# A two-block transformer kernel: the latent norms' scales moved behind the projections, the query rotation and one weight half moved in their queues

## The chip, the cores and the metric

The kernel runs on one core of a Trainium2 chip. The core has five engines that matter here: TensorE (PE in the rows; PEld is its weight load), VectorE (DVE), ScalarE (ACT), GpSimd (POOL) and the queue of SyncE (SP), which issues most DMAs. The metric is the device time of one execution in microseconds (us); lower is better. About 0.2% (5 us) is what a measurement of this kernel can tell from no change.

## The reference, cut to what matters

Two blocks are computed one after the other on 512 tokens of width 1024, in fp32. The first block has a forgetting attention ("fox", 8 heads), a stick-breaking attention (8 heads) and a mixture of 16 experts. The second block has two layers; the mixer of its first layer ("mixer a", the second mixer of the whole program) has a short convolution and a latent attention. Of mixer a the change touches this:

```python
proj = xn @ w_in
g_b, g_c, hv, c_q, c_kv, k_r = jnp.split(proj, [o1, o2, o3, o4, o5], axis=-1)
y_conv = g_b * short_conv(g_c * hv, conv_w)
q = (rms_norm(c_q, q_norm) @ w_q_up).reshape(b, s, MLA_HEADS, MLA_NOPE + MLA_ROPE)
q = jnp.concatenate([q[..., :MLA_NOPE], rope(q[..., MLA_NOPE:], pos)], axis=-1)
kv = (rms_norm(c_kv, kv_norm) @ w_kv_up).reshape(b, s, MLA_HEADS, MLA_NOPE + MLA_V)
k_rope = jnp.broadcast_to(rope(k_r[:, :, None, :], pos), (b, s, MLA_HEADS, MLA_ROPE))
```

with `rms_norm(x, g) = x * rsqrt(mean(x*x) + EPS) * g`. `c_q` has 768 features, `c_kv` 256, `k_r` 32. The root mean square is one number per token, and a projection sums over features, so it can be multiplied in before or behind the projection.

## The kernel before

Each engine has one instruction queue written out by hand; semaphores order the engines, and nothing is scheduled by a planner. PSUM has 8 banks, `PB[0]` to `PB[7]`, of 128 x 512 fp32. They are used as two sets, 0 to 3 and 4 to 7. A product of 512 x 512 outputs is a "group" with a running number; even groups write set 0, odd ones set 1. `acc_done` counts the groups that TensorE has completed, `acc_free[s]` the evictions of set s (ScalarE evicts set 0 and VectorE set 1 in most stages), and TensorE waits for it before it writes the set again (`await_set`).

Most products are made of split operands: a weight chunk arrives in `RING` by DMA, ScalarE casts half a chunk to its high part `WH` (`split` on ScalarE, line 893), VectorE subtracts to get the low part `WL` (`split` on VectorE, line 2376), and TensorE runs three matmuls for each pair of tiles (`split_group`, line 1578). Such a half chunk is called a part; a group has four parts of 24 matmuls. In both queues `upto(n)` issues the splits of the parts below n that are still to come. `WH` and `WL` have two buffers, so ScalarE casts part q when part q-1 has begun.

**The end of fox attention** (lines 2619 to 2657, and 1834 to 1841 on TensorE). TensorE computes group g+4 (parts 12 to 15). Behind part 14 it runs `last_spreads`: two matmuls that write the inverse softmax sums to `PB[7]`, one after the other, each followed by a gather on VectorE (`fox_gather`, line 2614). Then comes part 15. VectorE has in its queue: the low half of part 14, gathers 2 and 3, four multiply-adds of the modulation (`ada_part`), the low half of part 15, four more multiply-adds, and the low half of part 16, the first one of group g+5.

**Mixer a.** Its input projection has six groups: g to g+4 are split groups for `GBT`, `GCT`, `HVT` and the latents (g+3: tiles 0 to 3 of `CQ`; g+4: tiles 4 and 5 of `CQ` and both of `CKV`), feature-major, that is with tokens along the columns. Group g+5 is the 32 features of `k_r`: 64 plain fp32 matmuls of 32 columns into `PB[4]` (line 2066). Then comes the latent norm: ScalarE squares `CQ` and `CKV` into `SQ`; TensorE multiplies by a matrix of ones (lines 2074 and 2078), which leaves the sum over features in all 128 partitions, for 512 tokens along the columns; VectorE and ScalarE take mean, root and reciprocal on 128 x 512 tiles (`RT`), and VectorE scales the eight tiles in place, with the gain as a per-partition scalar (lines 2960 to 2969). `l_c` then lets TensorE start the projections `qup` (two groups) and `kvup` (two groups), whose outputs have tokens in the partitions (`QN`, `KVN`). `rope` rotates the queries in `QN` and VectorE's last eviction fills the second half of `KVN`; GpSimd copies the keys' parts from `KVN` and `KR2` to `KN` (lines 1476 to 1483). TensorE then transposes queries (`m = 0`) and keys (`m = 1`) by heads (line 2127), and VectorE and ScalarE evict them alternately. The attention loop `mla` follows.

A plain fp32 matmul has two records in the trace, a transpose or a split matmul has one.

## Time and profile before

| | us |
|---|---|
| median of 3 runs | 2497.91 (2496.5 to 2499.46) |
| the profiled execution, whole | 2497.15 |
| span of its trace | 2495.1 |
| TensorE busy in it | 2279.3 |
| VectorE busy | 1237.6 |
| ScalarE busy | 929.9 |
| GpSimd busy | 182.7 |

Times inside the trace count from the start of the span. The rest of the execution lies around it. The granted TensorE clock is given as a share of 2.4 GHz: 1.00 is 2.4 GHz, 0.50 is 1.2 GHz. The profile's chain of work goes back from the last instruction, at each step to what released it; where a wait is named after one engine, another may have come as late.

### The profile page before, as it was taken

The page shows a single profiled execution, that of the slowest core. Times are in us where ns is not written, and L with a number is a line of the kernel's source. Part 1 is how long each engine was busy: PE and PEld are TensorE (multiplying, and loading weights), DVE is VectorE, ACT ScalarE, POOL GpSimd, SP SyncE. Part 2 cuts the span into 40 slices and gives each one's busy share as a digit, 9 for nine tenths or more (in the row PEclk, how much of TensorE's full clock was granted, in tenths as well). Part 3 has the DMA queues.
Part 4 walks back from the last instruction along what each step waited for, and adds up shares of the span by engine and source line. Part 5 has one row for each costly group of instructions (what it writes and reads, how often), then busy time and mean ns, then how long its engine had stood idle before and what let it go on. Part 6 is the DMA issues. An engine that isn't in the chain of part 4 may idle for free.

```text
span 2495.1 us, 26080 instructions
## 1 busy us (share of the span) xinstructions
PE 2279.3 (91%) x10140; PEld 1712.4 (69%) x10140; DVE 1237.6 (50%) x1672; ACT 929.9 (37%) x1433; POOL 182.7 (7%) x222
## 2 busy tenths in 40 slices
PE   6898999987999959977889999989999997899998
PEld 4667667656666637845678888878855556788887
DVE  5735543256777744244554444453345545444544
ACT  3443531134555523203451224342255453312343
POOL 0330001101000010001000000020211200000000
PEclk9999899988999979978999999999899998999999
DMA  9303124827999952210123233232100002233221
GB/s 360 102 11 135 35 96 149 331 76 290 368 375 372 383 208 85 72 48 32 34 77 101 86 100 101 92 113 85 36 1 1 1 1 68 79 99 101 93 93 68
DMA packets 148459, 309.38 MB, mean 124 GB/s; under 512 B 17774, under 2 KB 19699, under 8 KB 148341
## 3 DMA queue, kind: packets, MB, share of 16 engines
q1 hardware_dynamic: 120468, 229.75, 27.0%
q10 hardware_dynamic: 16500, 36.62, 4.3%
q0 software_dynamic: 11376, 41.42, 4.2%
q8 instruction: 79, 1.29, 0.2%
q14 instruction: 36, 0.29, 0.0%
HBM read 276.56 MB, written 30.99 MB: 123 GB/s over the span
## 4 chain that ended last, share of the span: by engine, by line
PE 78%; DVE 10%; DMA 4%; ACT 4%; issue 3%; ACTq 0%; POOL 0%; DVEq 0%; POOLq 0%; SPq 0%; PEldq 0%
PE PB L1576 51%; PE PB L2020 4%; PE PB L2285 3%; DMA BIG<-in_expert_w_down 3%; PE PB L1561 2%; PE PB L2261 1%; DVE WL L2379 1%; PE PB L2089 1%; PE PB L2066 1%; PE PB L1802 1%; PE PB L2262 1%; DVE CI L3131 1%; PE PB L2224 1%; DVE X L2439 1%; PE PB L1723 1%
## 5 line engine op out<-in xcount | busy, mean ns | idle before, releaser
L2379 DVE TENSOR_TENSOR WL<-RING,WH 128x1024 fp32r<-128x1024 f32 x232 | 286.9, 1236 | 660.4 <-ACT WH L899 384.2
L899 ACT CAST WH<-RING 128x1024 fp32r<-128x1024 f32 x232 | 244.9, 1056 | 873.4 <-PE PB L1576 848.9
L1576 PE MATMUL PB<-HTH,WH 128*128 128x512 f32 x1056 | 416.8, 395 | 15.5 <-DVE WL L2379 9.7
L1576 PE MATMUL PB<-HTL,WH 128*128 128x512 f32 x1056 | 414.0, 392 | 0.0
L1576 PE MATMUL PB<-HTH,WL 128*128 128x512 f32 x1056 | 413.7, 392 | 0.0
L1576 PEld LDWEIGHTS PB<-HTH,WH 128*128 128x128 f32 x1056 | 200.3, 190 | 61.5 <-DVE WL L2379 12.1
L1576 PEld LDWEIGHTS PB<-HTH,WL 128*128 128x128 f32 x1056 | 200.1, 189 | 41.9
L1576 PEld LDWEIGHTS PB<-HTL,WH 128*128 128x128 f32 x1056 | 200.2, 190 | 41.6 <-issue 0.7
L1576 PE MATMUL PB<-WH,NHH 128*128 128x512 f32 x512 | 199.4, 390 | 1.8 <-DVE NHL L2382 1.8
L1576 PE MATMUL PB<-WH,NHL 128*128 128x512 f32 x512 | 199.2, 389 | 0.0
L1576 PE MATMUL PB<-WL,NHH 128*128 128x512 f32 x512 | 199.2, 389 | 0.0
L2746 DVE TENSOR_TENSOR EWL<-RING,EWH 128x1024 fp32r<-128x1024 f32 x128 | 151.8, 1221 | 59.7 <-ACT EWH L1093 59.5
L1576 PE MATMUL PB<-EWH,HTL 128*128 128x512 f32 x512 | 169.5, 413 | 3.9 <-DVE HTL L2888 3.9
L1093 ACT CAST EWH<-RING 128x1024 fp32r<-128x1024 f32 x128 | 130.6, 1049 | 92.1 <-PE PB L1576 70.7
L1576 PE MATMUL PB<-WH,HTH 128*128 128x512 f32 (+1 forms) x320 | 123.1, 385 | 23.7 <-DVE HTL L2382 16.0
L1576 PE MATMUL PB<-WH,HTL 128*128 128x512 f32 (+1 forms) x320 | 121.2, 379 | 0.0
L1576 PE MATMUL PB<-WL,HTH 128*128 128x512 f32 (+1 forms) x320 | 120.7, 377 | 0.0
L1576 PEld LDWEIGHTS PB<-EWH,HTL 128*128 128x128 f32 x512 | 95.8, 192 | 28.5 <-issue 6.7
L1576 PEld LDWEIGHTS PB<-WH,NHH 128*128 128x128 f32 x512 | 96.1, 188 | 22.5 <-DVE NHL L2382 2.6
L2020 PE MATMUL PB<-BIG,NAT 128*128 128x512 f32 x240 | 106.1, 594 | 4.8 <-DMA BIG<-in_expert_w_down 4.6
L1576 PEld LDWEIGHTS PB<-WL,NHH 128*128 128x128 f32 x512 | 96.1, 188 | 20.1
L1576 PEld LDWEIGHTS PB<-WH,NHL 128*128 128x128 f32 x512 | 96.1, 188 | 19.8
(497 smaller groups left out, 3491.1 us busy)
## 6 DMA issues: line engine op xcount, KB each, us to landing
RING<-in_mlp_w SPq DMA_DIRECT2D x64, 1024.0 KB, 5.2
RING<-in_expert_w_gate SPq DMA_DIRECT2D x32, 1024.0 KB, 7.4
RING<-in_expert_w_up SPq DMA_DIRECT2D x32, 1024.0 KB, 11.9
BIG<-in_expert_w_down ACTq DMA_DIRECT2D x15, 2048.0 KB
BIG<-in_ada_w SPq DMA_DIRECT2D x10, 2048.0 KB, 11.0
RING<-in_w_in SPq DMA_DIRECT2D x20, 1024.0 KB, 5.2
dispatch_rows<-BIG POOLq DMA_DIRECT2D x24, 512.0 KB, 16.0
RING<-in_a_w_in SPq DMA_DIRECT2D x10, 1024.0 KB, 5.1
```

What stands on the lines that cost most here:

```text
L899: ins = nc.scalar.copy(WH[:, q % 2], halves_of(n, q))
L1093: nc.scalar.copy(EWH[:, q % MOE_SLOTS], halves_of(CH["moe"] + GU_AT[e] + j // 2, j)).then_inc(high_ready, 1)
L1561: ins = pe.matmul(PB[4 * (g % 2) + b][:, :], lhs, rhs, start=(opens and m == 0 and k == 0), stop=(closes and m == chunks - 1 and k == KK - 1))
L1576: yield pe.matmul(dst, lhs, rhs, start=(start and n == 0), stop=(stop_ and n == 2))
L1723: ins = pe.matmul(PB[6 + u % 2][:, 0:DH], PT[0:n, u % 2, j, :], v(it, h, b, j, n), start=(j == 0), stop=(j == len(m) - 1))
L1802: ins = pe.matmul(PB[5 + h % 2][:, j * P:T], v, PROB[:, n % 4, 0:T - j * P], start=(j == 0), stop=(j == NT - 1))
L2020: ins = pe.matmul(PB[5 + m][:, :], ACTT[e % 2][:, k, :], w[:, k, :], start=(k == 0), stop=(k == KK - 1))
L2066: ins = pe.matmul(PB[4][:, i * 32:(i + 1) * 32], x[:, k, i * P:(i + 1) * P].bitcast(F32), SW[:, k, SW_KR:SW_KR + 32], start=(k == 0 and n ...
L2089: ins = pe.matmul(PB[b][:, :], CQ[:, k0 + k, b * P:(b + 1) * P], w[:, k, :], start=(m == 0 and k == 0), stop=(m == 1 and k == kk - 1))
L2285: ins = pe.matmul(dst, lhs, rhs, start=(j == 0), stop=last)
L2379: ins = V.tensor_tensor(WL[:, q % 2], halves_of(n, q), WH[:, q % 2].bitcast(F32), ALU.subtract)
L2746: V.tensor_tensor(EWL[:, q % MOE_SLOTS], halves_of(CH["moe"] + GU_AT[e] + j // 2, j), EWH[:, q % MOE_SLOTS].bitcast(F32), ALU.subtract).th ...
```

## The change

In mixer a, the latents are evicted from PSUM with their gain already multiplied in (`latents` on VectorE), and ScalarE squares the raw sums straight from PSUM (`latent_squares`). The per-token sums are no longer spread over all partitions: each of 32 matmuls takes 128 tokens of one tile of squares as the stationary operand and two columns of ones as the moving one, so that the sums come out with tokens in the partitions, all in `PB[5]`. Mean, root and reciprocal are taken on 128 x 8 numbers (`LSUM`, `LRMS`, `LRSTD`). The reciprocal root is multiplied in when the projections are evicted, as a per-partition scale (`evac` with `scale`, on both engines). TensorE starts `qup` when the latents have been evicted. In VectorE's queue `rope` of the queries now stands ahead of the eviction of the second `kvup` group. Near the end of fox attention the low half of part 15 is split ahead of gathers 2 and 3, and the release of the PSUM set stands ahead of the modulation's multiply-adds.

```diff
@@ ScalarE, mixer a
+            upto(18)
+            def latent_squares(m):
+                act.wait_ge(acc_done, g + 4 + m)
+                for b in range(4):
+                    ins = nc.scalar.activation(LSQ[:, 4 * m + b, :], PB[4 - 4 * m + b][:, :], ACT.Square)
+                ins.then_inc(l_sq, 1)
+            latent_squares(0)
             upto(20)
-            evac(g + 4, lambda b: CQ[:, 4 + b, :] if b < 2 else CKV[:, b - 2, :])
-            act.wait_ge(acc_free[0], (g + 4) // 2 + 1)
-            act.wait_ge(acc_free[1], (g + 4) // 2)
-            nc.scalar.activation(SQ[...][:, 0:6, :], CQ, ACT.Square).then_inc(l_sq, 1)
-            nc.scalar.activation(SQ[...][:, 6:8, :], CKV, ACT.Square).then_inc(l_sq, 1)
-            for m in range(2):
-                act.wait_ge(l_ms, m + 1)
-                nc.scalar.activation(RT[:, m, :], RT[:, m, :], ACT.Sqrt).then_inc(l_rms, 1)
-            evac(GR["qup"], lambda b: QN[:, b, 0:W])
-            evac(GR["kvup"], lambda b: KVN[:, b, 0:W])
+            latent_squares(1)
+            act.wait_ge(l_ms, 1)
+            nc.scalar.activation(LRMS, LSUM, ACT.Sqrt).then_inc(l_rms, 1)
+            act.wait_ge(l_c, 2)
+            evac(GR["qup"], lambda b: QN[:, b, 0:W], scale=lambda b: LRSTD[:, b:b + 1])
+            evac(GR["kvup"], lambda b: KVN[:, b, 0:W], scale=lambda b: LRSTD[:, NT + b:NT + b + 1])
@@ TensorE, mixer a
-            pe.wait_ge(acc_free[0], (g + 1) // 2)
-            pe.wait_ge(l_sq, 1)
-            for k in range(6):
-                ins = pe.matmul(PB[0][:, :], ONES[:, 0:P], sq[:, k, :], start=(k == 0), stop=(k == 5))
-            ins.then_inc(l_sum, 1)
             pe.wait_ge(l_sq, 2)
-            for k in range(2):
-                ins = pe.matmul(PB[1][:, :], ONES[:, 0:P], sq[:, 6 + k, :], start=(k == 0), stop=(k == 1))
+            for i in range(NT):
+                for at_, tiles in ((i, range(6)), (NT + i, (6, 7))):
+                    for k in tiles:
+                        ins = pe.matmul(PB[5][:, 2 * at_:2 * at_ + 2], LSQ[:, k, i * P:(i + 1) * P], ONES[:, 0:2],
+                                        start=(k == tiles[0]), stop=(k == tiles[-1]))
             ins.then_inc(l_sum, 1)
@@ VectorE, end of fox attention
-            upto(15)
+            upto(16)
             fox_gather(2)
             fox_gather(3)
-            ada_part(0, 3, ADA_ACC[4], 0, 4, fresh=True)
             dve.wait_ge(f_used, 4)
             dve.sem_inc(acc_free[1], 1)
-            upto(16)
+            ada_part(0, 3, ADA_ACC[4], 0, 4, fresh=True)
             ada_part(0, 3, ADA_ACC[4], 4, 4)
             upto(17)
@@ VectorE, mixer a
-            evac(g + 3, lambda b: CQ[:, b, :])
+            latents(0, [(CQ, "a_q_norm_2", k) for k in range(4)])
             upto(20)
...
+            latents(1, [(CQ, "a_q_norm_2", k) for k in (4, 5)] + [(CKV, "a_kv_norm_2", k) for k in (0, 1)])
+            dve.wait_ge(acc_free[0], (g + 4) // 2 + 1)
+            dve.sem_inc(l_c, 1)
+            dve.wait_ge(acc_done, g + 6)
+            V.tensor_copy(KRN.rearrange("p a b -> p (a b)"), PB[4][:, 0:NT * 32])
+            dve.wait_ge(l_sum, 1)
...
+            dve.wait_ge(l_ms, 1)
+            dve.sem_inc(acc_free[1], 1)
+            dve.wait_ge(l_rms, 1)
+            V.reciprocal(LRSTD, LRMS).then_inc(l_c, 1)
...
-            evac(GR["qup"] + 1, lambda b: QN[:, b, W:768], width=256)
-            evac(GR["kvup"] + 1, lambda b: KVN[:, b, W:D])
+            evac(GR["qup"] + 1, lambda b: QN[:, b, W:768], width=256, scale=lambda b: LRSTD[:, b:b + 1])
             dve.wait_ge(acc_free[0], GR["qup"] // 2 + 1)
+            dve.wait_ge(acc_free[1], (GR["qup"] + 1) // 2 + 1)
             rope(QN.rearrange("p t (h d) -> p t h d", h=MLA_H), MLA_H, None).then_inc(m_qn, 1)
+            evac(GR["kvup"] + 1, lambda b: KVN[:, b, W:D], scale=lambda b: LRSTD[:, NT + b:NT + b + 1])
```

Three places in the engines' queues. First VectorE at the end of fox attention, before; `WL<-RING,WH` is the low half of a part, `FOT<-FOT,PB` a gather, `NAT<-BIG,STAT` the modulation's multiply-adds:

```order
L2612 TENSOR_TENSOR FWT<-FSUMS,FWT 4x512 [waits dve_chain]
L2379 TENSOR_TENSOR WL<-RING,WH 128x1024 [waits high_parts_written]
L2617 TENSOR_TENSOR FOT<-FOT,PB 128x512 [waits fox_weights_spread] x2
L2358 TENSOR_SCALAR NAT<-BIG,STAT 128x512 [waits ada_pair_in0]
L2360 SCALAR_TENSOR_TENSOR NAT<-BIG,STAT,NAT 128x512 [waits dve_chain] x3
L2379 TENSOR_TENSOR WL<-RING,WH 128x1024 [waits dve_chain,fox_weights_used,high_parts_written]
L2360 SCALAR_TENSOR_TENSOR NAT<-BIG,STAT,NAT 128x512 [waits ada_pair_in0]
L2360 SCALAR_TENSOR_TENSOR NAT<-BIG,STAT,NAT 128x512 [waits dve_chain] x3
L2379 TENSOR_TENSOR WL<-RING,WH 128x1024 [waits high_parts_written]
```

The same place in the changed kernel:

```order
L2615 TENSOR_TENSOR FWT<-FSUMS,FWT 4x512 [waits dve_chain]
L2382 TENSOR_TENSOR WL<-RING,WH 128x1024 [waits high_parts_written] x2
L2620 TENSOR_TENSOR FOT<-FOT,PB 128x512 [waits fox_weights_spread] x2
L2361 TENSOR_SCALAR NAT<-BIG,STAT 128x512 [waits fox_weights_used,ada_pair_in0]
L2363 SCALAR_TENSOR_TENSOR NAT<-BIG,STAT,NAT 128x512 [waits dve_chain] x3
L2363 SCALAR_TENSOR_TENSOR NAT<-BIG,STAT,NAT 128x512 [waits ada_pair_in0,dve_chain]
L2363 SCALAR_TENSOR_TENSOR NAT<-BIG,STAT,NAT 128x512 [waits dve_chain] x3
L2382 TENSOR_TENSOR WL<-RING,WH 128x1024 [waits high_parts_written]
```

The low half of part 15 moved ahead of both gathers, and all eight multiply-adds now stand between the gathers and the low half of part 16.

Second, TensorE between the products for `k_r` and the first `qup` group, before:

```order
L2074 MATMUL PB<-NAT,ONES 128x512 [waits latent_squares,acc_free0]
L2074 MATMUL PB<-NAT,ONES 128x512 x5
L2078 MATMUL PB<-NAT,ONES 128x512 [waits latent_squares]
L2078 MATMUL PB<-NAT,ONES 128x512
L2089 MATMUL PB<-RING,BIG 128x512 [waits chunk_in_slot0,latent_normed,acc_free0]
```

And in the changed kernel:

```order
L2080 MATMUL PB<-ONES,NAT 128x2 [waits latent_squares]
L2080 MATMUL PB<-ONES,NAT 128x2 x31
```

Eight wide matmuls became 32 narrow ones; the `qup` products follow them at once, with `latent_normed` (`l_c`) already raised by the evictions of the latents.

Third, VectorE from the projections' evictions to the evictions of the transposed heads, before:

```order
L2453 COPY NAT<-PB 128x256 [waits acc_done,dve_chain]
L2453 COPY NAT<-PB 128x256 x3
L2453 COPY HT<-PB 128x512 [waits acc_done]
L2453 COPY HT<-PB 128x512 x3
L2982 TENSOR_TENSOR BIG<-NAT,COS 128x512 [waits acc_free0]
...
L2988 TENSOR_TENSOR NAT<-BIG 128x32x16 [waits dve_chain]
L3011 TENSOR_SCALAR BIG<-PB 96x512 [waits mla_transposed] x4
```

And in the changed kernel:

```order
L2458 TENSOR_SCALAR NAT<-PB,STAT 128x256 [waits acc_done,dve_chain]
L2458 TENSOR_SCALAR NAT<-PB,STAT 128x256 x3
L2995 TENSOR_TENSOR BIG<-NAT,COS 128x512 [waits acc_free1,acc_free0]
...
L3001 TENSOR_TENSOR NAT<-BIG 128x32x16 [waits dve_chain]
L2458 TENSOR_SCALAR HT<-PB,STAT 128x512 [waits acc_done]
L2458 TENSOR_SCALAR HT<-PB,STAT 128x512 x3
L3025 TENSOR_SCALAR BIG<-PB 96x512 [waits mla_transposed] x4
```

The seven steps of the rotation moved ahead of the four evictions into `KVN` (`HT`).

## Rows read from the trace of the kernel before

**Rows 1.** The page: busy time of each engine; the chain's shares by engine.
```profile
PE 2279.3 (91%) x10140; PEld 1712.4 (69%) x10140; DVE 1237.6 (50%) x1672; ACT 929.9 (37%) x1433; POOL 182.7 (7%) x222
...
PE 78%; DVE 10%; DMA 4%; ACT 4%; issue 3%; ACTq 0%; POOL 0%; DVEq 0%; POOLq 0%; SPq 0%; PEldq 0%
```

**Rows 2.** Chain of waits, fox's end: start us, us, engine, tile, line, count.
```profile
194.87 16.58 PE PB L1576 x72
...
212.55 0.49 PE PB L1781
...
216.68 1.24 DVE WL L2379
217.96 8.20 PE PB L1576 x24
```

**Rows 3.** Timeline of VectorE there: start us, us, line, operation, count, [idle before].
```profile
213.06 0.69 DVE L2617 TENSOR_TENSOR FOT<-FOT,PB 128x512 f32<-128x512 f32 x1 [0.66 <-PE PB L1781]
213.66 0.48 DVE L2358 TENSOR_SCALAR NAT<-BIG,STAT 128x512 f32<-128x512 f32 x1
214.18 2.33 DVE L2360 SCALAR_TENSOR_TENSOR NAT<-BIG,STAT,NAT 128x512 f32<-128x512 f32 x3
...
217.82 3.11 DVE L2360 SCALAR_TENSOR_TENSOR NAT<-BIG,STAT,NAT 128x512 f32<-128x512 f32 x4
```

**Rows 4.** Timeline of ScalarE there: the cast of part 15.
```profile
206.33 1.06 ACT L899 CAST WH<-RING 128x1024 fp32r<-128x1024 f32 x1 [4.38 <-PE PB L1576]
```

**Rows 5.** Windows there: length, busy PE, PEld, DVE, ACT, POOL, clock, DMA share, GB/s.
```profile
213.00:218.00 5.00, 0.06 (x2) 0.04 (x1) 4.66 (x7) 0.00 (x0) 0.00 (x0) 0.84 0.00 0
218.00:226.00 8.00, 8.00 (x25) 6.35 (x26) 3.96 (x5) 1.05 (x1) 0.00 (x0) 0.67 0.01 2
```

**Rows 6.** Chain of waits in mixer a, from the k_r products to the keys' transposes.
```profile
1050.67 22.11 PE PB L2066 x128
1072.78 7.17 PE PB L2074 x12
1079.95 1.72 PE PB L2078 x4
1081.67 12.90 issue
1094.57 23.75 PE PB L2089 x48
...
1128.68 13.75 PE PB L2111 x32
...
1142.45 2.48 DVE HT L2453 x4
...
1150.78 5.78 PE PB L2127 x32
...
1157.42 3.69 PE PB L2127 x32
```

**Rows 7.** A window in mixer a; columns as in rows 5.
```profile
1056.00:1072.50 16.50, 16.50 (x80) 16.50 (x79) 0.00 (x0) 0.52 (x1) 0.00 (x0) 0.50 0.00 1
```

**Rows 8.** Windows of 2 us where the clock rises again; columns as in rows 5.
```profile
1076.00:1078.00 2.00, 2.00 (x5) 0.91 (x4) 0.00 (x0) 0.00 (x0) 0.00 (x0) 0.86 0.00 0
...
1100.00:1102.00 2.00, 2.00 (x6) 0.87 (x5) 1.90 (x4) 0.00 (x0) 0.00 (x0) 0.89 0.51 207
```

**Rows 9.** Line 1629, two-column matmuls: min/median/max ns, first to last start us.
```profile
L1629 PE MATMUL PB<-ONES,SCORE x16: 251/251/272, 37.9 to 39.6; 128*128 128x2 f32 x16
```

**Rows 10.** Timeline of VectorE in mixer a: a reciprocal, and the convolution's end.
```profile
1082.31 3.34 DVE L2964 RECIPROCAL BIG<-BIG 128x512 f32<-128x512 f32 x1
...
1106.72 0.69 DVE L3002 TENSOR_TENSOR BIG<-BIG 128x512 f32<-128x512 f32 x1
```

**Rows 11.** GpSimd's two copies for the keys: min/median/max ns, first to last start us.
```profile
L1481 POOL COPY BIG<-HT x4: 922/1068/1074, 1145.1 to 1150.1; 128x512 f32<-128x512 f32 x4
...
L1482 POOL COPY BIG<-BIG x4: 397/718/855, 1146.0 to 1151.1; 128x256 f32<-128x256 f32 x4
```

More of the change, by code:

```diff
@@ L368, in program @@
     KRN, KR2, RT = big(10240, NT, 32), big(10368, NT, 32), big(10496, 3, 512)
-    OT2, SQ = big(6144, 4, T), NAT
+    OT2, LSQ = big(6144, 4, T), NAT[:, :, :].rearrange("p a (c b) -> p (a c) b", c=2)
     QN = NAT[:, :, :].rearrange("p a b -> p (a b)")[:, 0:NT * 768].rearrange("p (a b) -> p a b", a=NT)
@@ L677, in program @@
         PRMS, PRSTD, EPS2 = STAT[:, 50:54], STAT[:, 54:58], STAT[:, 49:50]
+        LSUM, LRMS, LRSTD = (STAT[:, 32 + 8 * i:40 + 8 * i] for i in (0, 1, 3))
         SQX = PT[:, :, :, :].rearrange("p a b c -> p (a b c)")
@@ L910, in evac @@
                 for b in range(banks):
-                    ins = nc.scalar.activation(dst(b), PB[b][:, 0:width], func, scale=scale)
+                    ins = nc.scalar.activation(dst(b), PB[b][:, 0:width], func, scale=scale(b) if callable(scale) else scale)
                 ins.then_inc(acc_free[0], 1)
@@ L2954, in _, with latents @@
             upto(18)
[L2955 to L2969 removed]
+            def latents(m, tiles):
+                dve.wait_ge(l_sq, m + 1)
+                for b, (dst, name, k) in enumerate(tiles):
+                    at_ = VEC_AT[name] + k
+                    ins = V.tensor_scalar(dst[:, k, :], PB[4 - 4 * m + b][:, :], COLS[:, at_:at_ + 1], None, ALU.mult)
+                ins.then_inc(acc_free[1 - m], 1)
+            latents(0, [(CQ, "a_q_norm_2", k) for k in range(4)])
+            upto(20)
+            latents(1, [(CQ, "a_q_norm_2", k) for k in (4, 5)] + [(CKV, "a_kv_norm_2", k) for k in (0, 1)])
[4 more added lines that the diff above has]
+            dve.wait_ge(l_sum, 1)
+            for m, rank in enumerate((Q_RANK, KV_RANK)):
+                ins = V.tensor_scalar(LSUM[:, m * NT:(m + 1) * NT], PB[5][:, 2 * m * NT:2 * (m + 1) * NT:2], 1.0 / rank, EPS,
+                                      ALU.mult, ALU.add)
+            ins.then_inc(l_ms, 1)
+            dve.wait_ge(l_ms, 1)
+            dve.sem_inc(acc_free[1], 1)
+            dve.wait_ge(l_rms, 1)
+            V.reciprocal(LRSTD, LRMS).then_inc(l_c, 1)
+            dve.wait_ge(l_c, 2)
             def rope(v, heads, out_):
```

16 lines of the change are left out of this document (1 added, 15 removed).

## The prediction

> **What bounds the kernel now.** I read the page first: TensorE is busy for 91% of the span, and the chain of work that ended last runs through it for 78% [rows 1]. So an edit on another engine counts only where TensorE waits for it. I then read the chain of waits in the two stretches that the change touches. Near the end of fox attention the reader is to see that the chain leaves TensorE: the second spread ends at 213.04, and part 15 starts only at 217.96, released by VectorE's low half [rows 2]. In mixer a there are two more holes: 12.90 us between the sums and the first `qup` product, and 8.3 us from the end of `kvup` (1142.4) to the first transpose (1150.78) [rows 6]. The windows of the same stretches are the third view: they show at which clock TensorE works beside these holes [rows 5, 7, 8].
>
> **Part 1, the weight half ahead of the gathers.** ScalarE's cast of part 15 is done at 207.4 [rows 4], while VectorE next has work only for gather 2, behind TensorE's part 14. So the subtraction of 1.24 us fits ahead of the gathers and costs nothing; part 15 can start when the second spread ends, at 213.0 instead of 217.96. It has 24 matmuls. Before, it ran mostly at 1.2 GHz, since TensorE had been idle for 4.9 us (granted clock 0.67 from 218 to 226), and took 8.20 us [rows 2, 5]. The 72 matmuls of the three parts ahead took 16.58 us, so 24 take 5.5 us at 2.4 GHz. Part 15 then ends at 218.5.
>
> What is late next: part 16. Its low half stands behind all eight multiply-adds now. They start at 213.7 behind gather 3 and take 0.48 + 2.33 + 3.11 = 5.9 us [rows 3], then the subtraction takes 1.24 [rows 2]: 220.9. ScalarE's cast for it waits only for part 15 to begin. Before, part 16 began when part 15 ended, at 226.16. So this edit gives 226.16 - 220.9 = 5.2 us, while TensorE idles for 2.4 us ahead of part 16. The lower bound: should the clock fall in that gap, part 16 costs what part 15 did, 8.20 - 5.5 = 2.7 us more, which leaves 2.5. I take 5.2, since the gap is half of the one in which it fell before. Behind it all engines and the weight loads are triggered by TensorE's progress, so I expect the shift to be kept.
>
> **Part 2, the sums and the norm.** Removed from TensorE's path are the wide sums, 7.17 + 1.72 us, and the hole of 12.90 us, in which VectorE took two reciprocals of 128 x 512 (3.34 us each [rows 10]) and scaled eight tiles. The sum of what goes is 21.8 us [rows 6].
>
> Added are 32 narrow matmuls, 64 records. Their price depends on the clock. The 64 products of 32 columns for `k_r` run just ahead: in the windows from 1056 to 1072.5 they have 80 records in 16.5 us, 0.206 us each, at a granted clock of 0.50, though TensorE is never idle [rows 7]. At 2.4 GHz the two-column matmuls of line 1629 have 15 spacings in 1.7 us, 0.113 us each [rows 9]. The moving side being 2 columns instead of 32, I expect no less work, since 32 and 2 columns cost the same at 2.4 GHz to within the rounding. So the new sums cost 64 x 0.206 = 13.2 us at 1.2 GHz (13.7 if a few of the 80 lie partly outside the window) and 7.2 us at 2.4 GHz. I take 13.4: the narrow stream ahead was at 1.2 GHz to its end, and this one is narrower. Thus `qup` starts at 1072.78 + 13.4 = 1086.2 instead of 1094.57: 21.8 - 13.4 = 8.4 us gained (8.1 to 8.6).
>
> The Trainium skill (TensorE: Matmul & The Clock Gate, LDWEIGHTS) says that a weight load takes a time that goes by the columns of the stationary tile alone, and this speaks against the change: each narrow matmul still loads 128 columns, four times as often as the eight wide ones did. The rows agree in that 2 columns cost 0.113 us each. By the page's figure of 128/1.2 ns = 107 ns for a load, an estimate of the 64 would be 6.8 us, half of what I take for the lower clock.
>
> Work that leaves other queues' paths: ScalarE squares eight banks from PSUM and VectorE evicts with the gain. For g+3 this lies beside group g+4; for g+4 it lies beside the 22.11 us of `k_r` products. The mean, root and reciprocal on 128 x 8 numbers are tiny. The rotation of `k_r` and the convolution, which ended at 1107.4, 12.8 us behind the norm [rows 6, 10], now start at about 1087.5 and end at about 1101, ahead of the first `qup` eviction (1110). Without that cover, an eviction would be late by the part of the 12.8 us that sticks out. The set 1 banks are released when VectorE has read the sums, at about 1087, and the second `qup` group needs them 23 us later.
>
> `qup` itself took 23.75 us, of which the first 5.6 ran at 1.2 GHz: the clock rose inside the window from 1100 to 1102 [rows 6, 8]. In the sums before, it rose inside the window from 1076 to 1078, 3.7 us behind the first wide matmul [rows 8]. The new `qup` also starts at 1.2 GHz. I take no difference (bounds 0 and 1 us gained).
>
> **Part 3, the rotation ahead of the last eviction.** Call K the end of `kvup`. Before, VectorE evicted for 2.5 us behind K and then rotated; the transposes of the queries began at K+8.4 and those of the keys at K+15.0 [rows 6]. Now the rotation (5.9 us, from 1144.9 to 1150.8) lies beside the 13.75 us of `kvup` [rows 6]. The transposes of heads 0 to 3 start at K (0.46 us a head, 3.69 / 8), those of heads 4 to 7 behind the eviction, which is still at K+2.5 to K+2.8, and they are all evicted at about K+5.7. Then the keys: GpSimd's eight copies cannot start before the eviction has ended, as before (K+2.7). Before they took 6.45 us, from 1145.1 to 1151.5, and were hidden; now they are what ends last. The four 256-wide ones took 0.855 us beside VectorE's steps and 0.397 at the end without them [rows 11]. So the copies take 4 x 1.0 + 4 x 0.4 = 5.6 us now, when VectorE reads PSUM or rests (upper bound 6.45), and the keys' transposes start at K+8.5 (8.3 to 9.2) instead of K+15.0: 6.5 us.
>
> The Trainium skill (SBUF — State Buffer, Who interferes with whom) has a rule for this: a VectorE instruction with two SBUF inputs contends with a GpSimd instruction that reads SBUF, one with at most one does not. The trace agrees with its 0.855 and 0.397. Without the rule the copies would keep their 6.45 us, and the keys would start at K+9.2.
>
> The clock takes some of it back. TensorE idles from K+4.8 to K+8.5, so that I expect it to fall to 1.2 GHz around the keys' transposes. The same 32 transposes took 3.69 us at full clock and 5.78 us for the queries, mostly at the lower one [rows 6]: 2.1 us more, upper bound 3.7 (the double). So part 3 gives 6.5 - 2.1 = 4.4 us (2.1 to 6.5).
>
> **The sum** is 5.2 + 8.4 + 4.4 = 18.0 us. Against the profiled execution's span, 2495.1 becomes 2477.1, and the whole execution, 2497.15, 2479.2. The median of the runs is 0.8 us above that execution: 2497.9 - 18.0 = 2479.9.
>
> **Rivals.** *The clock falls twice more* (chance 0.20): in the 2.4 us ahead of part 16, and for all of the keys' transposes. It costs 2.7 + 1.6 us: 2484.2. For it: the clock is down after every idle stretch of 5 us or more. Against: here they are 2.4 and 3.7 us.
>
> *The clock comes sooner* (0.15): no fall around the keys, and `qup` at full speed 1 us earlier. That is 2.1 + 1 us less: 2476.8.
>
> *The narrow sums run at 2.4 GHz* (0.05): 64 x 0.113 = 7.2 us instead of 13.4, and `qup` without its slow start, 2.8 us less: 2479.9 - 9.0 = 2470.9. Against it stand the `k_r` products, back to back and at 0.50 [rows 7]. The Trainium skill (TensorE: Matmul & The Clock Gate, Loop structure matters more than you think) has matmuls that stay back to back stay at the full clock, which would lead here; this trace disagrees for narrow ones.
>
> *The change does not do what it says* (0.03): the holes only move, because the multiply-adds hold part 16 longer than worked out or the KN copies start late; less than 5 us is left, 2493 or more.
>
> *Slower* (0.03): one long run at the lower clock. With the hole gone, nothing separates the narrow stream from the projections, and if 1.2 GHz stayed granted through `qup` and `kvup`, they would take twice their full-clock time (21 + 10.4 + 13.7 us, of which 2.8 are lost already): 42 us more, 2522. It decides from 36 us more of the lower clock on. Against it: both wide streams of the rows were back at full clock 4 to 6 us after they began, one of them straight behind `k_r` [rows 8].
>
> My forecast as worked out holds 0.54 (2477.5 to 2482.5).
>
> **How the numbers follow.** The range for 8 in 10 takes in the forecast, the two clock cases and the bounds of the single terms: least gain 2.5 + 8.1 + 2.1 = 12.7 (2485.2), most 5.2 + 8.6 + 6.5 + 1 = 21.3 (2476.6); with about 1 us for the scatter of the median it is 2475.5 to 2486. Faster by over 0.2% (5 us; a measurement of this kernel can tell no less from no change): 0.94. Within 0.2%: 0.03. Slower: 0.03.
>
> **What would show it.** Part 1: part 15 starts at once behind the second spread, part 16 about 2.4 us after part 15's end, at clock 1.00. Part 2: 64 narrow records in 13 to 14 us at 0.50, `qup` at once behind, about 8.4 us sooner after the `k_r` products than before. Part 3: first transpose at K, GpSimd's copies some 5.6 us long, keys' transposes at K+8.5. Wrong would be: records of 0.11 us in the sums, a fall of the clock in part 16, an eviction of `qup` that waits for the convolution, or a later stretch that gives the shift back.

## The result, and the profile after

| | before | after |
|---|---|---|
| median of 4 runs, us | 2497.20 | 2472.27 (2470.48 to 2476.08) |
| ratio | | 0.9902, 95% interval 0.9889 to 0.9916 |
| the profiled execution, us | 2497.15 | 2476.08 |
| span of its trace, us | 2495.1 | 2474.0 |

The changed kernel is 24.9 us faster; the prediction was 2479.9, at least 2475.5. The direction and the three gains were as predicted; the size was larger, and the median lies 3.2 us below the range. The two profiled spans differ by 21.1 us, so 3.8 us of the 24.9 are not in this pair of profiles.

The page of the changed kernel answers to [rows 1]. Where line numbers differ from the rows of before, the operation and the tile name the same step: split matmuls L1582, `k_r` L2072, sums L2080, `qup` L2092 and L2102, `kvup` L2114, head transposes L2130.

```profile
PE 2274.8 (92%) x10188; PEld 1716.3 (69%) x10188; DVE 1225.9 (50%) x1667; ACT 925.4 (37%) x1434; POOL 180.4 (7%) x222
...
PE 79%; DVE 9%; DMA 5%; ACT 4%; issue 2%; POOL 1%; ACTq 0%; DVEq 0%; POOLq 0%; SPq 0%; PEldq 0%
```

TensorE has 48 records more and 4.5 us less busy time; GpSimd, which was at 0% of the chain, has 1%. That last point is the one that the prediction missed: a wait for GpSimd is now on the path.

**End of fox attention.** The chain of waits of the changed kernel (start us, us, engine, tile, line), which answers to [rows 2, 3]:

```profile
215.25 0.48 PE PB L1787
...
217.11 0.76 DVE NAT L2363
...
222.59 1.14 DVE WL L2382
...
223.87 8.19 PE PB L1582 x35
```

Its windows, which answer to [rows 5] (length, busy PE, PEld, DVE, ACT, POOL, clock, DMA share, GB/s):

```profile
213.00:218.00 5.00, 4.13 (x19) 3.10 (x18) 2.71 (x5) 1.05 (x1) 0.00 (x0) 1.00 0.13 50
218.00:223.00 5.00, 3.20 (x15) 2.31 (x13) 4.82 (x7) 1.74 (x3) 0.00 (x0) 1.00 0.00 0
```

The second spread ends at 215.73 and TensorE goes on at once with part 15; the chain runs along VectorE's multiply-adds to part 16 at 223.87. The clock is 1.00 through the whole place, where it was 0.84 and 0.67. This execution was 2.7 us later than that of before when it came here, and nearly all of that from near its start (the first matmul of L1748, ahead of fox attention, began at 95.0; its like of before at 92.4), so 223.87 compares with 226.16 + 2.7: 5.0 us gained. From the last spread to the first scores of the stick-breaking attention it took 53.0 us instead of 58.3: 5.3.

**Mixer a.** The chain of waits there, which answers to [rows 6]:

```profile
1068.12 13.61 PE PB L2080 x64
1081.72 23.02 PE PB L2092 x48
1104.75 10.36 PE PB L2102 x48
1115.11 13.75 PE PB L2114 x32
1128.88 2.74 DVE HT L2458 x4
...
1134.50 0.55 POOL BIG L1487
...
1135.39 6.63 issue
...
1142.46 1.02 POOL QS L1427
...
1143.74 2.43 PE PB L1708 x6
```

The 12.90 us of "issue" ahead of `qup` are gone. At the end of the stage there is a new "issue" of 6.63 us, between GpSimd's last copy for the keys and its copy of the first heads (`QS`), which the attention loop needs.

TensorE, VectorE and GpSimd behind K, the end of `kvup` (1128.88), in the timeline of the changed kernel; it answers to [rows 11]:

```profile
1131.75 0.61 POOL L1487 COPY BIG<-HT 128x512 f32<-128x512 f32 x1 [120.90 <-DVE HT L2458]
1132.31 0.39 POOL L1488 COPY BIG<-BIG 128x256 f32<-128x256 f32 x1
...
1135.45 3.70 PE L2130 MATMUL PB<-IDENT,BIG 128*96 128x128 f32 x32 [1.83 <-POOL BIG L1488]
...
1139.18 0.69 DVE L3027 COPY BIG<-PB 96x512 f32<-96x512 f32 x1 [0.19 <-PE PB L2130]
...
1142.43 1.04 POOL L1427 COPY QS<-BIG 96x1024 f32 x1 [7.04 <-POOLq L258]
```

The keys' transposes start at K+6.6 and take 3.70 us, at full clock. The last eviction ends at 1139.9, but `QS` starts 2.6 us later, released by line 258. That line is GpSimd's drain, in the helper `meet`, in which all engines wait for each other ahead of the attention loop (one line of before and one of after, min/median/max ns and first start):

```profile
L258 POOLq DRAIN  x3: 41/988/12749, 1145.3 to 2002.6; - x3
```
```profile
L258 POOLq DRAIN  x3: 41/987/9936, 1132.0 to 1981.7; - x3
```

The drain starts with the copies, at 1132.0, and its 9.9 us end at about 1142, some 6.5 us behind the last of them. Before, its 12.7 us from 1145.3 also ended 6.5 us behind the last copy (1158.0 against 1151.5), but there the transposes and evictions covered it: `QS` then started at 1162.3, 0.5 us behind the last eviction.

Where the 21.1 us between the two spans lie, from the starts of TensorE's groups: up to the last spread -2.7 (later); from there to the stick-breaking scores 5.3; to the experts' first down product 1.3; through the experts to the `k_r` products 0.4; from these to the last transpose behind the latent attention (called the last head transpose below) 16.4 (172.8 us to 156.4); behind it 0.4. Of the 16.4, 8.5 are the sums and the norm (start of `k_r` to start of `qup`, 43.9 to 35.4 us), 0.7 `qup`, 6.3 the way from K to the first matmul of the loop (21.2 to 14.9 us), and 0.8 the loop.

### The profile page after: what moved, and what is told of

Read it like the earlier page. It is cut to its first block, busy times and chain, and to the rows that moved or that the text cites. A ratio compares the mean times of both kernels' runs of the same rounds, so it can differ in the third digit from the quotient of the medians.

```text
span 2474.0 us, 26175 instructions
## 1 busy us (share of the span) xinstructions
PE 2274.8 (92%) x10188; PEld 1716.3 (69%) x10188; DVE 1225.9 (50%) x1667; ACT 925.4 (37%) x1434; POOL 180.4 (7%) x222
## 4 chain that ended last, share of the span: by engine, by line
PE 79%; DVE 9%; DMA 5%; ACT 4%; issue 2%; POOL 1%; ACTq 0%; DVEq 0%; POOLq 0%; SPq 0%; PEldq 0%
PE PB L1582 51%; PE PB L2026 4%; PE PB L2288 3%; DMA BIG<-in_expert_w_down 3%; PE PB L1567 2%; PE PB L2264 1%; DVE WL L2382 1%; PE PB L2092 1%; PE PB L2072 1%; PE PB L1808 1%; PE PB L2265 1%; DVE CI L3145 1%; PE PB L2227 1%; DVE X L2442 1%; DVE NAT L2363 1%
## 5 line engine op out<-in xcount | busy, mean ns | idle before, releaser
L1582 PE MATMUL PB<-HTH,WH 128*128 128x512 f32 x1056 | 416.3, 394 | 13.3 <-DVE WL L2382 7.6
L1582 PE MATMUL PB<-HTL,WH 128*128 128x512 f32 x1056 | 413.7, 392 | 0.0
L1582 PE MATMUL PB<-HTH,WL 128*128 128x512 f32 x1056 | 413.5, 392 | 0.0
L1582 PEld LDWEIGHTS PB<-HTH,WH 128*128 128x128 f32 x1056 | 200.1, 189 | 58.3 <-issue 10.9
L1582 PEld LDWEIGHTS PB<-HTL,WH 128*128 128x128 f32 x1056 | 200.1, 189 | 42.0 <-issue 0.7
L1582 PEld LDWEIGHTS PB<-HTH,WL 128*128 128x128 f32 x1056 | 199.9, 189 | 41.9
L1582 PE MATMUL PB<-WH,NHH 128*128 128x512 f32 x512 | 199.4, 389 | 1.7 <-DVE NHL L2385 1.7
L1582 PE MATMUL PB<-WH,NHL 128*128 128x512 f32 x512 | 199.2, 389 | 0.0
L1582 PE MATMUL PB<-WL,NHH 128*128 128x512 f32 x512 | 199.2, 389 | 0.0
L2748 DVE TENSOR_TENSOR EWL<-RING,EWH 128x1024 fp32r<-128x1024 f32 x128 | 151.6, 1219 | 59.8 <-ACT EWH L1094 59.7
L1582 PE MATMUL PB<-EWH,HTL 128*128 128x512 f32 x512 | 169.2, 412 | 3.9 <-DVE HTL L2890 3.9
L1582 PE MATMUL PB<-WH,HTH 128*128 128x512 f32 (+1 forms) x320 | 122.8, 384 | 23.6 <-DVE HTL L2385 16.0
L1582 PE MATMUL PB<-WH,HTL 128*128 128x512 f32 (+1 forms) x320 | 120.9, 378 | 0.0
L1582 PE MATMUL PB<-WL,HTH 128*128 128x512 f32 (+1 forms) x320 | 120.7, 377 | 0.0
L1582 PEld LDWEIGHTS PB<-EWH,HTL 128*128 128x128 f32 x512 | 95.2, 191 | 28.6 <-issue 6.7
L1582 PEld LDWEIGHTS PB<-WH,NHH 128*128 128x128 f32 x512 | 96.1, 188 | 22.5 <-DVE NHL L2385 2.6
L1582 PEld LDWEIGHTS PB<-WL,NHH 128*128 128x128 f32 x512 | 96.1, 188 | 20.1
L1582 PEld LDWEIGHTS PB<-WH,NHL 128*128 128x128 f32 x512 | 96.1, 188 | 19.7
```

What stands on the lines that cost most here:

```text
L1582: yield pe.matmul(dst, lhs, rhs, start=(start and n == 0), stop=(stop_ and n == 2))
L2748: V.tensor_tensor(EWL[:, q % MOE_SLOTS], halves_of(CH["moe"] + GU_AT[e] + j // 2, j), EWH[:, q % MOE_SLOTS].bitcast(F32), ALU.subtract).th ...
```

## The experiments

Theory: the three parts save what they saved in the trace, 5 + 9 + 6 to 7 us, and what goes beyond that in the first comparison is scatter in stretches that the change doesn't touch. Rivals: the parts help each other; the narrow sums cost something else than their length; GpSimd's drain holds back the third part. Kernels under one heading marked "same chip" were compared on one chip, with runs of the kernel before between them; the three groups below ran on three different chips.

**The change again, and its three parts alone (same chip).** The whole is the changed kernel. The other three are the kernel before with one part of the diff. Of fox, alone:

```diff
-            upto(15)
+            upto(16)
             fox_gather(2)
             fox_gather(3)
-            ada_part(0, 3, ADA_ACC[4], 0, 4, fresh=True)
             dve.wait_ge(f_used, 4)
             dve.sem_inc(acc_free[1], 1)
-            upto(16)
+            ada_part(0, 3, ADA_ACC[4], 0, 4, fresh=True)
```

The norm alone is the whole change with this place, and the order of `rope` and the last eviction, as before. The rotation alone:

```diff
-            evac(GR["kvup"] + 1, lambda b: KVN[:, b, W:D])
             dve.wait_ge(acc_free[0], GR["qup"] // 2 + 1)
+            dve.wait_ge(acc_free[1], (GR["qup"] + 1) // 2 + 1)
             rope(QN.rearrange("p t (h d) -> p t h d", h=MLA_H), MLA_H, None).then_inc(m_qn, 1)
+            evac(GR["kvup"] + 1, lambda b: KVN[:, b, W:D])
```

> The whole change again, to size the total. The profile of the changed kernel accounts for 20.6 us from the four gaps (5.1 at the end of fox attention, 8.5 at the sums, 0.7 in the first projection, 6.3 from the end of the projections to the attention loop). Theory (the parts add up and nothing else moved): 20 to 22 us below the kernel before on the same chip, ratio 0.9912 to 0.9920; the 24.9 us of the first comparison was then partly scatter of the medians. Rival (something outside the four gaps gives 3 to 4 us more): 24 to 25 us again, ratio about 0.990.

> The kernel before with the weight half of part 15 ahead of the gathers, and nothing else. Theory: part 15 starts at once behind the second spread and part 16 waits for the eight multiply-adds; 5.0 to 5.3 us faster, ratio 0.9979. Rival (the shift is given back by a later stage): 0 to 2 us. Rival (it is the source of the unexplained rest): 8 to 9 us.

> The kernel before with the latent norm's change alone: the rotation stays behind the last eviction, and the weight half behind the gathers. Theory: 64 narrow records in 13.6 us at clock 0.50, the projection at once behind; 8.5 + 0.7 = 9.2 us faster, ratio 0.9963. From the end of the projections to the attention loop it should take 21.2 us as before, with GpSimd's copies slow beside the rotation (about 1.0 us for the wide ones, 0.8 for the narrow ones). Rival (it is the source of the unexplained rest): 12 to 13 us.

> The kernel before with the queries' rotation ahead of the last eviction, and nothing else. Theory: GpSimd's copies take 0.60 and 0.39 us each, 3.6 us in all, since VectorE no longer has two operands in SBUF beside them; the keys' transposes start 6.6 us behind the projections' end instead of 15.0, GpSimd's drain ends 6.5 us behind its last copy and holds the attention loop until 14.9 us behind that end instead of 21.2: 6.3 us faster, ratio 0.9975. The prediction's own step had 4.4 us. Rival (the clock falls around the keys' transposes): 4 us.

| kernel (before: 2497.01, 22 runs) | median us | less than before | ratio, 95% interval | `k_r` to last head transpose |
|---|---|---|---|---|
| whole | 2483.10 (2477.62 to 2485.92) | 13.9 | 0.9943 (0.9930 to 0.9956) | 158.5 |
| fox alone | 2492.10 (2485.67 to 2500.03) | 4.9 | 0.9981 (0.9969 to 0.9994) | 173.0 |
| norm alone | 2487.27 (2482.06 to 2489.01) | 9.7 | 0.9957 (0.9945 to 0.9969) | 162.0 |
| rotation alone | 2490.74 (2486.87 to 2497.58) | 6.3 | 0.9975 (0.9965 to 0.9985) | 165.4 |

Each part alone is faster than before, by a median near what its place in the trace shows, and they add up to 20.9 us; the interval of each is about 3 us to either side. The parts don't help each other: in mixer a, norm and rotation alone save 10.8 and 7.4 us, both together 14.3 here and 16.4 in the three other profiles of the whole, so 2 to 4 us less than their sum. But the whole was only 13.9 us faster here, 11 less than in the first comparison and less than the 20 to 22 expected. At its own place fox alone does what part 1 said. The chain of that kernel:

```profile
219.77 1.14 DVE WL L2379
...
221.05 14.12 PE PB L1576 x61
```

Part 16 starts at 221.05; the prediction had worked out 220.9. In the total the same profile kept nearly nothing of it: the execution took 2496.97 us, its span 2494.9 against 2495.1. It began the stick-breaking scores at 265.5 us instead of 270.9, but the experts' first down product at 612.7 instead of 613.8. The stretch from the last stick-breaking product to that down product, first with fox alone, then before (length, busy engines, clock, DMA):

```profile
328.50:612.70 284.20, 251.01 (x965) 179.73 (x964) 122.07 (x196) 78.78 (x106) 29.28 (x44) 0.91 0.55 197
```
```profile
334.70:613.80 279.10, 247.72 (x966) 177.35 (x964) 121.23 (x196) 78.10 (x105) 29.37 (x44) 0.93 0.55 200
```

The eleven runs fall apart by their mean clock: five at 0.948 or 0.949 took 2485.67 to 2492.10 us, six at 0.943 to 0.945 took 2491.15 to 2500.03. The profiled one is of the six. It fits that the median of 4.9 us stands between executions that keep the gain and executions that give most of it back (the other ten have no profile), and its nearness to 5.2 is then partly luck. The rival "the shift is given back by a later stage" is true of the profiled execution.

GpSimd's timeline with the rotation alone, and with the norm alone (the rotation behind the eviction, as before):

```profile
1147.60 0.60 POOL L1481 COPY BIG<-HT 128x512 f32<-128x512 f32 x1
1148.15 0.39 POOL L1482 COPY BIG<-BIG 128x256 f32<-128x256 f32 x1
...
1156.49 1.04 POOL L1421 COPY QS<-BIG 96x1024 f32 x1 [7.04 <-POOLq L258]
```
```profile
1141.83 1.07 POOL L1487 COPY BIG<-HT 128x512 f32<-128x512 f32 x1
1142.85 0.59 POOL L1488 COPY BIG<-BIG 128x256 f32<-128x256 f32 x1
```

So it is the place of the rotation that sets the copies' length, 0.60 or 1.07 us for the same instruction. The rotation itself gets shorter too: its second step took 0.98 us before (1145.57) and 0.69 us in the kernel with the rotation alone. The Trainium skill (SBUF — State Buffer, Who interferes with whom) says that a VectorE instruction with two SBUF inputs contends with a GpSimd instruction that reads SBUF. The traces agree with it for the wide copies as well as for the small ones. But the rotation's one copy step, which has a single SBUF input, was slowed too, 0.72 us beside GpSimd's copies and 0.43 without, so the prediction's "one with at most one does not" is too wide.

**The drain, and the price of the narrow sums (same chip).** The whole once more; the whole without GpSimd's drain ahead of the loop, where GpSimd waits for its own last copy by semaphore instead:

```diff
-            meet(pool, "pool")
+            pool.wait_ge(m_kn, 1 + NT)
+            meets["pool"] = 1
+            pool.sem_inc(met, 1)
+            pool.wait_ge(met, 4)
```

The whole with all 32 sums computed twice:

```diff
-            for i in range(NT):
+            for again in range(2):
+              for i in range(NT):
```

And the whole with the narrow products mixed into `qup`: 24 of them go ahead, and three stand behind each of the 24 wide matmuls of the first `qup` group.

```diff
+            some(24)
...
                         ins = pe.matmul(PB[b][:, :], CQ[:, k0 + k, b * P:(b + 1) * P], w[:, k, :],
                                         start=(m == 0 and k == 0), stop=(m == 1 and k == kk - 1))
...
+                        some(3)
```

> The whole change a third time, since the two comparisons gave 24.9 and 13.9 us and the parts apart 4.9 + 9.7 + 6.3 = 20.9. Theory (executions of one program differ by where the clock's falls land in the stretch around the routing, from 330 to 620 us, and the first microseconds; the change's own four gaps are the same each time): the median lies between 2470 and 2486, and in the profile the stretch from the first k_r product to the end of the heads' transposes is 14 to 17 us shorter than the 172.8 us of the kernel before. Rival (the whole is faster than its parts by an interaction in mixer a): that stretch differs between profiles by more than the clock's low periods in it explain.

> The changed kernel, with GpSimd's drain ahead of the attention loop replaced by a wait on its own last copies. In the changed kernel that drain ends 6.5 us behind the last copy, at 14.9 us less 1.8 behind the projections' end, and the loop's first copy waits for it; all others are there 2.3 us sooner. Theory (the drain took the place of the wait that was removed): the loop starts 2.2 us sooner, 2 us faster than the whole change of this call. Rival (GpSimd is late for another reason, such as the fetch of its instructions): no difference, the gap ahead of the copy into QS stays.

> The changed kernel, with the order of TensorE's matmuls changed between the input projection and the query projection: 24 of the 96 narrow matmuls (64 for k_r, 32 for the sums) first, then three of them behind each of the 24 wide ones of the first qup group. Same matmuls, same waits. Theory (a stretch of narrow matmuls alone makes the clock fall, wide ones between them hold it up): clock 1.00 throughout, the 96 narrow ones take 96 x 0.224 = 21.5 us and the wide ones 20.7, so 42 us in place of 58.4 us from the first k_r product to the end of that group; 15 to 16 us faster than the whole change. Rival (the clock falls here anyway, as it goes by the share of narrow matmuls): up to 84 us, 26 us slower.

> The changed kernel with its 32 narrow sums done twice (the second overwrites the first). Theory (each costs two records of 0.213 us at 1.2 GHz, all on TensorE's path): 13.6 us slower than the whole change, 27.2 us for 128 records at clock 0.50. Rival (part of the sums is hidden, since the projection waits for something else too): less than 10 us.

| kernel (before: 2495.87, 23 runs) | median us | less than before | ratio, 95% interval |
|---|---|---|---|
| whole | 2477.04 (2473.99 to 2480.35) | 18.8 | 0.9925 (0.9909 to 0.9941) |
| without the drain | 2479.56 (2475.01 to 2483.13) | 16.3 | 0.9931 (0.9913 to 0.9948) |
| three narrow behind each wide one | 2498.91 (2457.26 to 2506.89) | -3.0 | not given, its 12 runs are of two kinds |
| sums twice | 2491.28 (2484.40 to 2496.42) | 4.6 | 0.9975 (0.9963 to 0.9988) |

*Sums twice* costs 14.2 us against the whole. The chain of waits shows why:

```profile
1069.12 27.26 PE PB L2081 x128
1096.38 23.17 PE PB L2093 x48
```

128 records in 27.26 us, 0.213 us each, twice the 13.61 us, and `qup` starts at once behind. So the narrow sums cost their length, at the lower clock, and nothing behind them.

*Without the drain* the tail got shorter in the trace. K is at 1134.96 there:

```profile
1141.55 3.71 PE PB L2133 x32
...
1146.49 1.02 POOL QS L1427
1147.77 0.93 PE PB L1711 x4
```

The loop starts at K+12.8 instead of K+14.9: the 2 us are there, so the drain did hold the loop back. One of them is lost again in the loop, which took 59.8 us from its first matmul to the last head transpose instead of 58.9, with a clock of 0.83 instead of 0.91 in its first 20 us. The median doesn't show the rest; it is 2.5 us worse than the whole, with overlapping runs, where 2 us better was expected. In its profile the windows of the experts' routing differ from those of the whole on the same chip (first the whole, then without the drain):

```profile
500.00:620.00 120.00, 93.90 (x426) 70.86 (x425) 74.77 (x139) 53.09 (x73) 11.59 (x11) 0.90 0.55 194
```
```profile
500.00:620.00 120.00, 95.64 (x412) 71.34 (x411) 71.57 (x135) 50.53 (x71) 11.00 (x11) 0.85 0.51 181
```

Up to there the two are the same program, and it ran at a clock of 0.90 or 0.85, depending on where the falls land. This window was read in eight profiles: four have 0.89 or 0.90, and four, the kernel before among them, 0.84 to 0.86. As it is fixed in time and the kernels are not, the length of the stage says more. From the last stick-breaking product to the first down product it took 277.8 to 279.1 us in nine of all fourteen profiles, and 281.4 to 284.2 in the other five. The nine reached the stage (the last stick-breaking product) at 330.3 us or later, the five at 329.8 or earlier, and all five have the fox edit. So the executions that come there earliest give 3 to 6 us back. No run moves the time of arrival alone, so that it is the cause is not shown. Half of the ten profiles with the fox edit and none of the four without it have the long stage: a gain of 2 us cannot be told from this in six runs. Whether the drain costs 2 us in the total is left open.

*Three narrow behind each wide one* was expected to be 15 to 16 us faster than the whole, with a clock of 1.00. Its median is 21.9 us slower: the prediction's rival "slower" made real. The clock in its windows:

```profile
1043.00:1053.00 10.00, 10.00 (x61) 8.00 (x60) 2.73 (x4) 2.06 (x4) 0.00 (x0) 0.77 0.18 52
1053.00:1070.00 17.00, 17.00 (x47) 11.32 (x48) 0.00 (x0) 0.00 (x0) 0.00 (x0) 0.50 0.08 32
1070.00:1090.00 20.00, 20.00 (x56) 13.28 (x56) 0.29 (x1) 0.00 (x0) 0.00 (x0) 0.50 0.00 0
1090.00:1110.00 20.00, 20.00 (x54) 12.77 (x53) 0.00 (x0) 0.00 (x0) 0.00 (x0) 0.50 0.16 53
```

Through the 57 us from 1053 to 1110 TensorE was never idle and had 1.2 GHz. The clock fell at the end of the 24 narrow products that go ahead (0.61 in the window 1048 to 1050; the first wide matmul began at 1048.2, 5.3 us behind the first narrow one), and the mixture did not bring it back. One of the 12 runs took 2457.26 us at a mean clock of 0.957 instead of 0.937 to 0.942. It has no profile; the clock alone suggests that in it the mixture ran at 2.4 GHz. The same program went both ways here.

**Without fox, and the narrow products among the split ones (same chip).** The whole a fourth time; the whole with the fox place as before; and two kernels in which a part of the 64 `k_r` products stands inside group g+4, one behind two of three wide matmuls (48 of them), or behind one of three (24), in the last three of its four parts:

```diff
+                                if between is not None and m > 0:
+                                    between((m - 1) * 24 + b * 6 + k * 3 + n)
...
+            def between(at_):
+                if at_ % 3 < 2:
+                    next(narrow, None)
```

`narrow` is a generator that issues the `k_r` products one by one, with the wait for set 1 ahead of the first; with 24, the 2 is a 1. The rest follows group g+4, and then the sums, as in the whole.

> The change as it is, a fourth time, as the partner of the others on this chip. If the differences between the earlier comparisons of it (13.9, 18.8 and 24.9 us) are scatter of the stretches that it does not touch: 2472 to 2484, and from the first record of line 2072 (1576 or 2066 as before) to the last head transpose 155 to 159 us, against 172.8 in the kernel before. If the gain in mixer a itself varied, that stretch would differ by 5 us or more.

> Only the second and the third part of the change: the order at the end of fox attention is that of the kernel before. If the fox edit is worth its 5 us in every run, this is 4 to 6 us slower than the whole on this chip, and 14 to 16 us faster than the kernel before. If most of the fox edit is taken back further on, in the stretch from 330 to 620 us, where the clock falls fall differently, it is within 2 us of the whole. Stretch from the k_r products to the last head transpose: 155 to 159 us in both theories.

> The whole change, but 48 of the 64 k_r products stand one by one behind two of every three wide matmuls in the last three parts of the last split group; 16 products and the 32 sums stay behind. If two narrow products to three wide matmuls leave the clock at 1.00, each product costs 2 x 0.113 us instead of 0.345 us and the narrow stream behind is 96 records long instead of 192, of which the first 4 us run at full clock: 10.8 + 4 + 12.6 = 27.4 us instead of 35.7, so 8 us faster than the whole. If such a mixture also pulls the clock down (as 3 narrow to 1 wide did), the 72 wide matmuls take up to 16 us more and the projections may start slowly too: 8 us slower than the whole, or more.

> As the one before, with one narrow product behind every third wide matmul: 24 of 64 between the wide ones, 40 behind. If the clock holds: 24 x 0.226 = 5.4 us instead of 8.3, so 3 us faster than the whole, and no fall before the last wide matmul. If even this pulls the clock down: 8 us or more slower. If it holds here and falls with 48 between, the share of narrow products decides; if it falls in neither or in both, a share in this range does not.

| kernel (before: 2497.82, 11 runs) | median us | less than before | ratio, 95% interval | last down product to last head transpose |
|---|---|---|---|---|
| whole | 2476.30 (2472.98 to 2480.18) | 21.5 | 0.9915 (0.9901 to 0.9929) | 303.7 |
| without the fox edit | 2483.41 (2477.67 to 2484.61) | 14.4 | 0.9940 (0.9926 to 0.9955) | 303.6 |
| 48 between | 2470.19 (2464.65 to 2470.68) | 27.6 | 0.9892 (0.9877 to 0.9906) | 295.6 |
| 24 between | 2476.23 (2473.08 to 2484.11) | 21.6 | 0.9918 (0.9902 to 0.9933) | 303.4 |

*Without the fox edit* it is 7.1 us slower than the whole in the medians, so here the fox edit keeps its worth; the two profiled executions, 2479.58 and 2480.65 us, differ by only 1.1. Its chain has part 15 late and slow again, as before:

```profile
219.19 1.24 DVE WL L2382
220.48 8.15 PE PB L1582 x24
```

Both profiles have the short stage ahead of the first down product. Behind it the shift does not stay whole. At the last stick-breaking product the kernel without the edit is 5.5 us behind, at the first down product 5.9 and at the last one 3.1: the experts' stretch took 292.8 us in the one and 290.0 in the other. Over the fourteen profiles it took 287 to 294 us, without a relation to the edits.

*48 between* is the fastest, faster than the whole by 6.1 us, and by 8.1 in the stretch from the last down product to the last head transpose. Its windows in the mixture and behind it:

```profile
1035.00:1040.00 5.00, 5.00 (x33) 4.48 (x33) 0.00 (x0) 0.47 (x1) 0.00 (x0) 1.00 0.00 0
...
1050.00:1055.00 5.00, 5.00 (x33) 4.48 (x32) 0.00 (x0) 0.00 (x0) 0.00 (x0) 1.00 0.00 0
1055.00:1060.00 5.00, 5.00 (x42) 4.76 (x40) 0.53 (x1) 2.06 (x4) 0.00 (x0) 1.00 0.02 3
1060.00:1065.00 5.00, 5.00 (x31) 5.00 (x31) 2.49 (x5) 0.00 (x0) 0.00 (x0) 0.62 0.00 0
1065.00:1070.00 5.00, 5.00 (x25) 5.00 (x25) 0.00 (x0) 0.00 (x0) 0.00 (x0) 0.50 0.00 0
```

And its chain behind the mixture:

```profile
1057.34 3.49 PE PB L2074 x32
1060.83 13.12 PE PB L2098 x64
1073.95 22.93 PE PB L2110 x48
```

Two narrow products among three wide matmuls left the clock at 1.00. The 27.3 us from 1030.07 to 1057.34 hold 72 wide matmuls and 48 products; 72 wide ones alone take 16.6 [rows 2], so the 48 products cost 10.7 us, 0.22 us each. With 3.49 and 13.12 that is 27.3 us of narrow work instead of 21.77 + 13.61 = 35.4; 27.4 was expected.

*24 between* gained nothing that can be seen, though the clock held in its mixture too. Its 40 products behind took 14.36 us (80 records), so 24 products went from 7.4 us to about 5.4. Of these 2 us TensorE lost about 0.5 waiting for set 1 ahead of the first product and `qup` took 0.5 us more than in the whole. What remains is about 1 us, and 3 us were expected.

## Why the prediction was right, and where it was wrong

All three gains came from where the prediction had them. Two of its steps failed. Part 3 was put at 4.4 us and measured 6.3, and the range allowed "about 1 us for the scatter of the median", where medians of the same change differ by up to 11 us. The first alone would not have led out of the range: with the places as measured, 20.8 us, the forecast would have been 2497.9 - 20.8 = 2477.1.

*Part 1, 5.2 us:* right at its place. Part 15 at once, part 16 at the clock 1.00 and 5.0 us earlier; with this part alone it began at 221.05, worked out 220.9. The rival of a fall in the gap did not happen (2.66 us here). Wrong was the step "I expect the shift to be kept", given without a row: with this part alone the profiled execution had only 1.1 us of it left at the first down product.

*Part 2, 8.4 us:* right, 8.5 in the trace. The price of the sums was taken from the `k_r` products, 0.206 us a record; they cost 0.213, and twice as many cost twice as much. The rival with 2.4 GHz is refuted: of the 192 records back to back, the first 54 or so came every 0.11 us, and the other 138 at 0.50. The Trainium skill (TensorE: Matmul & The Clock Gate, Loop structure matters more than you think) has matmuls that stay back to back stay at the full clock; for these narrow ones the measurement decides against it. `qup` had been taken at no gain, bounds 0 and 1; it was 0.7 us shorter.

*Part 3, 4.4 us:* the mechanism is right, the size is not, 6.3. Three of its terms failed:

- The copies took 3.64 us, not 5.6. The step took about 1.0 us as the wide copy's own duration, with only the small ones slowed by VectorE. But all four wide ones of [rows 11] had lain beside the rotation, and the contention holds for them too: 0.60 us without it. So the keys started at K+6.6, not K+8.5.
- The fall of the clock around the keys' transposes, priced at 2.1 us, did not come: they took 3.70 us. TensorE's gap ahead of them was 1.8 us, with the shorter copies, instead of 3.7. That the shorter gap is why was not tested, and the prediction's argument by the length of the gap ("after every idle stretch of 5 us or more") was weaker than it reads: in the kernel before the clock was also down behind one of 2.4 us (0.50 in the 5 us from 134.8).
- Against both, GpSimd's drain was not seen: the 1.9 and 2.1 us gained on the sum would have made 8.4, and it kept 2.1 of them (K+12.8 without it, K+14.9 with it). The prediction stopped reading at the keys' transposes [rows 6]. It asked what is late next for part 1, and not for the end of this part.

So the three parts with `qup` gave 5.3 + 8.5 + 0.7 + 6.3 = 20.8 us in the profiled pair, with 0.8 in the attention loop 21.6, against the sum of 18.0. The medians of the parts measured alone add up to 20.9. The working was short by about 3 us.

*The range:* this is the second error, and the one that put the result outside. The whole was compared four times: 24.9, 13.9, 18.8 and 21.5 us less than before, mean 19.8; its medians were 2472.3, 2483.1, 2477.0 and 2476.3, those of before 2495.9 to 2497.8. Three of the four medians lie in the predicted range, the first does not. So a median of four to six runs of this kernel moves by 5 us either way between comparisons, and the first was a low draw; the profiled execution of that very comparison, 2476.08, was 3.8 us above its median. That the sum of 18.0 is near the mean of 19.8 is no proof of its terms, since 3 us of errors lie within this scatter. What moves the medians is shown in part, over the fourteen profiles: the start of the program (2.8 us), the stage ahead of the first down product (277.8 to 284.2 us), the experts' stretch (287 to 294 us), and what lies behind the last head transpose (1267.9 to 1272.2 us). The second of these goes with the time of arrival, which part 1 moves. The comparisons of the whole also differ in the chip, and whether the chip has a part in it was not tested. In the second comparison five of the six runs had a mean clock of 0.945 or 0.946, where the first had 0.947 to 0.950; its one profile (span 2478.7) lost 2 us in mixer a and 4 in the routing. Why nearly all of its runs were so is open.

## What to carry to other kernels

A short duration read in a trace belongs to its neighbours: before using it behind a move, look at what ran beside each of the rows it comes from, and whether it still will. When a move shortens the end of a stage, read on to the first instruction of the next stage, and through each engine's barrier: a drain that had been covered may be what comes late. A gain early in a kernel is not the same gain at its end: follow one profile to a later stage to see whether the shift is still there. Narrow matmuls that must be issued are cheapest among wide ones, in a mixture for which a run has shown that the clock stays up; and a range needs the scatter between comparisons, not that within one.

## What was not expected of the hardware

- GpSimd's drain ended about 6.5 us behind its last copy (issue of 6.63 us in the chain, the same in every kernel with the rotation ahead and the drain in place).
- The contention of VectorE and GpSimd goes both ways: GpSimd's copies took 0.60 or 1.07 us and 0.39 or 0.85 us, the rotation's second step 0.69 or 0.98 us.
- The lower clock does not need an idle TensorE. 64 products of 32 columns (from 4.3 to 5.9 us behind their start on, in the kernels that have them in one piece), the 32 of 2 columns behind them, and three such ones to a wide one of plain fp32, all without a gap, ran at 0.50; one or two narrow ones to three wide ones of the split kind ran at 1.00. The two mixtures differ also in what went ahead (48 narrow records in the one, wide ones in the other) and in the kind of the wide ones, so the share alone is not shown to decide.
- The same program took 2457.26 us once and 2492.91 to 2506.89 us eleven times.
- An execution that came to the experts' routing 6.2 us earlier left it only 1.1 us earlier (fox alone: 328.5 instead of 334.7 us, and 612.7 instead of 613.8).
